# Keys' turn, scaled activations and head outputs kept in PSUM, and two weight tiles opened together, at the seams of a two-block transformer kernel

## The reference, cut to what matters

```python
# layer a: differential attention, 8 heads of 2*128
q, k, v, gate = split(rms_norm(x, a_norm) @ a_w_in, 4);  q, k = partial_rope(q), partial_rope(k)
w = softmax(q0 k0) - lam * softmax(q1 k1)
o = rms_norm(w @ v, subln) * (1 - lambda_init) * silu(gate)
x = x + o @ a_w_out
# shared keys and values, then layer b: window attention with sinks, 32 query heads, 4 key heads
k, v = split(rms_norm(x, kv_norm) @ w_kv, 2);  k = partial_rope(k)
q, gate = split(rms_norm(x, b_norm) @ b_w_in, 2);  q = partial_rope(q)
o = sink_softmax(q k) @ v
x = x + (o * silu(gate)) @ b_w_out
# second block: three branches, then
mix = (g_a * (y_a @ w_a) + g_b * (y_b @ w_b) + g_c * (y_c @ w_c)) @ w_out      # "mix_out"
```

## Time and profile before

| | before |
|---|---|
| median of 3 runs | 2703.34 us |
| the profiled execution: its own time | 2707.28 us |
| its span in the profile | 2705.2 us |
| busy PE / DVE / ACT / POOL | 2604.6 / 997.0 / 1205.1 / 1889.8 us |
| granted PE clock, mean | 0.979 |
| moved by DMA | 425.62 MB, 157 GB/s |

### The profile page before, as it was taken

How to read it: one execution, slowest core, us unless ns; L and a number is a source line. 1 busy time by engine, 2 the same in 40 slices (tenths; PEclk the granted TensorE clock), 3 DMA queues, 4 the chain that set the end, 5 groups by cost and what they waited for, 6 DMA issues and landing times.

```text
span 2705.2 us, 57178 instructions
## 1 busy us (share of the span) xinstructions
PE 2604.6 (96%) x23930; PEld 2519.5 (93%) x23930; DVE 997.0 (37%) x1394; ACT 1205.1 (45%) x1435; POOL 1889.8 (70%) x786
## 2 busy tenths in 40 slices
PE   6999999998999999999999999999799999999996
PEld 5999999898998999999898999999699999999996
DVE  3444444326666341124434443250431130220412
ACT  3444444454666655444434352433343343443432
POOL 3766677676665787556566665888388888888884
PEclk8999999999999999899999999999899999999998
DMA  4555455454444566444444444566266666666663
GB/s 166 155 150 149 148 155 154 130 171 132 135 148 133 165 186 204 138 131 142 131 143 144 130 146 120 171 202 185 74 186 185 182 187 187 186 184 184 182 188 105
DMA packets 120024, 425.62 MB, mean 157 GB/s; under 512 B 12672, under 2 KB 18944, under 8 KB 119552
## 3 DMA queue, kind: packets, MB, share of 16 engines
q1 hardware_dynamic: 115104, 416.54, 51.9%
q10 hardware_dynamic: 4704, 5.77, 0.7%
HBM read 418.07 MB, written 4.19 MB: 156 GB/s over the span
## 4 chain that ended last, share of the span: by engine, by line
PE 92%; DVE 4%; ACT 2%; issue 1%; DMA 0%; SPq 0%; ACTq 0%; DVEq 0%
PE ps L218 20%; PE ps L220 20%; PE ps L227 20%; PE ps L272 16%; PE ps L1814 3%; PE ps L263 3%; PE ps L259 2%; PE ps L258 2%; PE ps L1107 2%; ACT wh L199 1%; DVE og L376 1%; DVE hl L304 1%; PE ps L790 1%; PE ps L1706 1%; PE ps L1708 1%
## 5 line engine op out<-in xcount | busy, mean ns | idle before, releaser
L2529 POOL TENSOR_TENSOR wl<-raw,wh 128x1024 fp32r<-128x1024 f32 x782 | 1889.6, 2438 | 781.3 <-ACT wh L199 780.7
L199 ACT ACTIVATE wh<-raw 128x2048 fp32r<-128x2048 f32 x391 | 748.0, 1913 | 667.9 <-PE ps L227 430.6
L218 PE MATMUL ps<-hh,wh 128*128 128x256 f32 (+1 forms) x3184 | 793.1, 287 | 30.8 <-DVE hl L304 26.6
L220 PE MATMUL ps<-hl,wh 128*128 128x256 f32 (+1 forms) x3184 | 789.2, 286 | 0.0
L218 PEld LDWEIGHTS ps<-hh,wh 128*128 128x128 f32 x3184 | 607.0, 191 | 37.8 <-issue 20.0
L220 PEld LDWEIGHTS ps<-hl,wh 128*128 128x128 f32 x3184 | 608.8, 191 | 0.0
L227 PE MATMUL ps<-hh,wl 128*128 128x256 f32 (+1 forms) x3184 | 418.1, 284 | 0.0
L227 PEld LDWEIGHTS ps<-hh,wl 128*128 128x128 f32 x3184 | 399.5, 189 | 0.0
L218 PE MATMUL ps<-gh,wh 128*128 128x256 f32 x1264 | 303.2, 281 | 0.0
L220 PE MATMUL ps<-gl,wh 128*128 128x256 f32 x1264 | 302.9, 281 | 0.0
L218 PEld LDWEIGHTS ps<-gh,wh 128*128 128x128 f32 x1264 | 239.1, 189 | 0.6 <-issue 0.6
(11 more groups left out here) (374 smaller groups left out, 2949.4 us busy)
## 6 DMA issues: line engine op xcount, KB each, us to landing
raw<-weights SPq DMA_DIRECT2D x782, 512.0 KB, 3.6
xT<-tokens SPq DMA_DIRECT2D x1, 2176.0 KB, 8.7
spill<-xT ACTq DMA_DIRECT2D x1, 2048.0 KB, 14.3
xT<-spill ACTq DMA_DIRECT2D x1, 2048.0 KB, 8.9
out<-xT SPq DMA_DIRECT2D x1, 2048.0 KB, 7.5
C<-consts SPq DMA_DIRECT2D x1, 2000.0 KB, 11.9
arena<-lora ACTq DMA_DIRECT2D x4, 384.0 KB, 3.2
P<-params SPq DMA_DIRECT2D x1, 125.0 KB, 12.8
```

The source lines that it names most:

```text
L199: nc.scalar.activation(wh[:, m % 2, :, :].rearrange("p a b -> p (a b)"), raw[:, 2 * (m % 2):2 * (m % 2) + 2, :, :].rearrange("p a b c -> p ...
L218: nc.tensor.matmul(acc[0:m, 0:n], wh[:, slot, kt, 0:m], rh[:, kt, 0:n], start=(kt == kts[0]), stop=False)
L220: nc.tensor.matmul(acc[0:m, 0:n], wh[:, slot, kt, 0:m], rl[:, kt, 0:n], start=False, stop=False)
L2529: nc.gpsimd.tensor_tensor(wl[:, s // 2, h, :], raw[:, s, :, :], wh[:, s // 2, h, :].bitcast(F32), ALU.subtract)\
```

## The change

1. **Two tiles open each output product** (`a_out`, `b_out`, `mix_out`). `opening_two` issues feature blocks 0 to 11 of tile 0, the same of tile 1 (in bank 1), then blocks 12 to 15 of tile 0 and of tile 1. For `mix_out` it replaces the plain tile.
2. **End of layer a.** `o` is written in place in PSUM, and `og` is made from PSUM. In the last head DVE subtracts quarter 1 before sqs, and quarter 2 right after var. ACT's order is as it was.
3. **`kv` to `b`.** The scaled activations go to PSUM (`Standing`: banks 4 and 5 for quarters 0, 2 and 3, banks 2 and 3 for quarter 1), so L304 subtracts from PSUM. The keys are turned in PSUM banks 0 and 1, the sine table lies in bank 6. Quarter 2 is subtracted before the shuffle and quarter 3 after the turn. ACT makes all copies to `kd`. New waits: `kv` tiles 2 and 3 on l1, quarters 2 and 3 of `gain` on l0 and l2, `b` tile 0 on radd.
4. **Last step of layer b.** PE issues the whole gate tile, then feature blocks 0 to 7 of tile 0 of `b_out`, before the transposes, and blocks 8 to 11 after them. DVE multiplies the gate (`gate`) before it needs the exponentials; ACT does Silu and the rounding of `b_out` tile 1 before its copy of the transposed weights (`wx`). Steps wx, g and gate get semaphores of their own.

```diff
+        def opening_part(pe, phase_name, t, acc, rh, rl, n, split, kts):
+            q = FIRST[phase_name] + t
+            pe.wait_ge(hi_done, q + 1)
+            for kt in kts:
+                if kt % split.size == 0:
+                    pe.wait_ge(split.V.sem, split.V.at(f"l{kt // split.size}"))
+                nc.tensor.matmul(acc[:, 0:n], wh[:, q % 2, kt, :], rh[:, kt, 0:n], start=(kt == 0), stop=False)
+                nc.tensor.matmul(acc[:, 0:n], wh[:, q % 2, kt, :], rl[:, kt, 0:n], start=False, stop=False)
+            for kt in kts:
+                if kt % 8 == 0:
+                    pe.wait_ge(lo_done, 2 * q + kt // 8 + 1)
+                ins = nc.tensor.matmul(acc[:, 0:n], wl[:, q % 2, kt, :], rh[:, kt, 0:n], start=False,
+                                       stop=(kt == 15))
+            return ins
+        def opening_two(pe, phase_name, accs, rh, rl, n, split, begun=False):
+            for kts in (range(12), range(12, KT)):
+                for t, acc in enumerate(accs):
+                    if begun and t == 0 and kts[0] == 0:
+                        continue
+                    ins = opening_part(pe, phase_name, t, acc, rh, rl, n, split, kts)
+                    if kts[-1] == KT - 1:
+                        ins.then_inc(tile_done, 1)
@@ attn_a_dve, last head @@
                 if ends:
                     split_ao.quarter_dve(dve, 0)
+                    split_ao.quarter_dve(dve, 1)
                 dve.wait_ge(A.sem, A.at("sqo", i))
...
                 if ends:
-                    split_ao.quarter_dve(dve, 1)
+                    split_ao.quarter_dve(dve, 2)
...
-                if ends:
-                    split_ao.quarter_dve(dve, 2)
-                        out=fa["o"][:, d, :], in0=ps[:, 6 + d, 0:NT], scalar=p("subln", d), in1=fa["rstd"],
+                        out=ps[:, 6 + d, 0:NT], in0=ps[:, 6 + d, 0:NT], scalar=p("subln", d), in1=fa["rstd"],
@@ kv_pe, tiles 2 and 3 @@
+                    pe.wait_ge(split_b.V.sem, split_b.V.at("l1"))
@@ gain in kv_act @@
+                if k >= 2:
+                    act.wait_ge(split_b.V.sem, split_b.V.at("l0" if k == 2 else "l2"))
+                    ins = nc.scalar.activation(gained[k][:, j, :], xT[:, kt, 0:SEQ], ACT.Copy, scale=p("b", kt))
@@ kv_dve @@
+            turned, sine = ps[:, 0:2, 0:NT], ps[:, 6, 0:NT]
+            nc.vector.tensor_tensor(sine, c("sin_b"), factor_b.out, ALU.mult)
             split_b.quarter_dve(dve, 1)
+            split_b.quarter_dve(dve, 2)
...
-            nc.vector.tensor_tensor(sh, sh, both(f2["sinr"]), ALU.mult)
+            nc.vector.tensor_tensor(sh, sh, both(sine), ALU.mult)
-            nc.vector.tensor_tensor(x, x, both(f2["cosr"]), ALU.mult)
+            nc.vector.tensor_tensor(turned, turned, both(f2["cosr"]), ALU.mult)
-            nc.vector.tensor_tensor(x, x, sh, ALU.add)
+            nc.vector.tensor_tensor(x, turned, sh, ALU.add)
-            for e in range(2):
-                kd_copy(nc.vector.tensor_copy, V, 0, e)
-            split_b.quarter_dve(dve, 2)
             split_b.quarter_dve(dve, 3)
@@ attn_b_pe @@
-                for k in range(4):
+                for k in range(6 if ends else 4):
+                    ins = part(pe, "b", n, k, ps[:, 1, :], hh, hl, SEQ)
+                if ends:
+                    ins.then_inc(tile_done, 1)
+                    opening_part(pe, "b_out", 0, ps[:, 0, :], gh, gl, SEQ, split_bo, range(8))
...
+                if ends:
+                    opening_part(pe, "b_out", 0, ps[:, 0, :], gh, gl, SEQ, split_bo, range(8, 12))
```

More of the change, by code:

```diff
@@ L306, in dve, with __init__, quarter_act, quarter_dve @@
                         .then_inc(self.V.sem, self.V.step(f"l{k}"))
+        class Standing(Split):
+            def __init__(self, name, places, pair, n):
+                Split.__init__(self, name, None, pair, n)
+                self.places = places
+            def quarter_act(self, eng, V, count, k):
+                f = slice(4 * k, 4 * k + 4)
+                eng.wait_ge(V.sem, count)
+                nc.scalar.activation(self.pair[0][:, f, 0:self.n], self.places[k], ACT.Copy)\
+                    .then_inc(self.A.sem, self.A.step(f"h{k}"))
+            def quarter_dve(self, eng, k):
+                f = slice(4 * k, 4 * k + 4)
+                eng.wait_ge(self.A.sem, self.A.at(f"h{k}"))
+                nc.vector.tensor_tensor(self.pair[1][:, f, 0:self.n], self.places[k],
+                                        self.pair[0][:, f, 0:self.n].bitcast(F32), ALU.subtract)\
+                    .then_inc(self.V.sem, self.V.step(f"l{k}"))
         class Norm:
@@ L1040, in kv_act @@
                     act.wait_ge(V.sem, V.at("radd"))
-                    for e in range(2):
-                        kd_copy(lambda o, i_: nc.scalar.activation(o, i_, ACT.Copy), A, 1, e)
+                    for h in range(2):
+                        for e in range(2):
+                            kd_copy(lambda o, i_: nc.scalar.activation(o, i_, ACT.Copy), A, h, e)
         def kv_dve(dve):
@@ L1242, in attn_b_dve, with gate @@
             dve.wait_ge(SK["v"].sem, SK["v"].at("table"))
+            def gate(s):
+                dve.wait_ge(tile_done, done("b", 2 + 2 * s - (s == STEPS_B - 1)))
+                nc.vector.tensor_tensor(f2["gb"][:, s % 2, :], ps[:, 1, 0:256], f2["rs"][:, 0:256], ALU.mult)\
+                    .then_inc(SGB["v"].sem, SGB["v"].step("gate"))
             for s in range(STEPS_B):
+                ends = s == STEPS_B - 1
                 at = P_AT["sinks"][0] + 2 * s
@@ L1262, in attn_b_dve @@
                     .then_inc(V.sem, V.step("sn"))
+                if ends:
+                    gate(s)
                 dve.wait_ge(A.sem, A.at("es", s))
@@ L1278, in attn_b_dve @@
                     .then_inc(V.sem, V.step("w2"))
-                dve.wait_ge(tile_done, done("b", 2 + 2 * s - (s == STEPS_B - 1)))
-                nc.vector.tensor_tensor(f2["gb"][:, s % 2, :], ps[:, 1, 0:256], f2["rs"][:, 0:256], ALU.mult)\
-                    .then_inc(V.sem, V.step("gate"))
+                if not ends:
+                    gate(s)
                 if s in (6, 10, 14):
@@ L1288, in attn_b_dve @@
             split_bo.quarter_dve(dve, 3)
-        b_out = Product("b_out", "b_out", (gh, gl), SEQ, xT, add=True, split=split_bo, after="zz")
+        b_out = Product("b_out", "b_out", (gh, gl), SEQ, xT, add=True, split=split_bo, after="zz",
+                        begun=True)
         two = TwoNorms("two", ("fin", "mix_pre"), SEQ, b_out.blocks(),
```

78 lines of the change are left out of this document (44 added, 34 removed).

## The result

| | before | after |
|---|---|---|
| median | 2703.39 us (4 runs, 2701.4 to 2706.2) | 2677.45 us (4 runs, 2675.5 to 2678.8) |
| the profiled execution: its own time | 2707.28 us | 2678.78 us |
| its span | 2705.2 us | 2676.9 us |
| busy PE / DVE / ACT / POOL | 2604.6 / 997.0 / 1205.1 / 1889.8 | 2594.4 / 978.5 / 1205.8 / 1886.4 |
| granted PE clock, mean | 0.979 | 0.985 |

The ratio of after to before is 0.9901, with a 95% interval of 0.9889 to 0.9914: 25.9 us faster by the medians, 28.3 by the two spans. Forecast were 27.0 us and 2676.3 us.

A forecast was written before the change was run, and what follows sets the result against it. PE was taken as the bound (92% of the chain), plus its stops and half clock. Gains 11.1 + 6.9 + 6.2 + 3.0 = 27.2, less 0.2, give 27.0 off 2703.34: 2676.3 us, range 2671.5 to 2682.5.

The forecast's parts named there:

- The first rival: DVE and POOL still exclude each other with PSUM forms: kv to b gains only 4.4 us, total 2683.0 us; 6%.
- the term for the product with the values: Last step of layer b: the product with the values takes half of 2.64 us, ending at 878.5.
- The longer wait for sqs: End of layer a: PE waits 3.4 instead of 1.19 us, as quarter 1's subtraction now precedes sqs.
- The clock's loss: End of layer a: half clock after PE's stop loses 1.5 to 3.3 us, taken as 2.0.
- the third rival: End of layer a gains nothing, its longer stop and cold start eating 3 us: total 2679.3 us; 8%.
- the lower bound: End of layer a: if the 3.4 us stop counts as a cold start, the gain is 1.7 us.
- The wait for ACT at the third tile: At each two-tile opening PE waits 0.7 to 0.9 us for ACT's rounding of tile 2's upper weights.
- the wait for POOL's second half: Tile 2's second half comes from POOL 4.8 us after the upper part against PE's 4.7: 0.2 us off the sum.
- The second rival: Tile 2 of each product waits for POOL, up to 2.4 us three times: gain 20, total 2683.5 us; 6%.
- the refill loop: Slower rival: weight slots' refill (10.6 us per two tiles against PE's 11.3) becomes the bound; at 6 us landing 2712; 3%.

The follow-up runs named there:

- kv_sbuf: Changed kernel with scaled activations, turned keys and sine table back in SBUF between kv and b, new order and ACT copies kept: 2676.33 us (5 runs).
- a_order: Changed kernel with the subtraction of quarter 1 at the end of layer a moved behind sqs, before var: 2674.47 us (4 runs).
- kv_both: Changed kernel with activations, keys' turn and sine in SBUF and the first half of the kd copies on DVE before quarter 3: 2686.23 us, one run.
- no_fill: Changed kernel with the last step of layer b as before the change, b_out still opened by two tiles: 2684.47 us (7 runs).
- mix_one: Changed kernel with mix_out opened by one plain tile as before the change: 2683.79 us (9 runs).
- a_one: Changed kernel with a_out opened by one plain tile, DVE's new order kept: 2681.53 us, one run.
- best2: Changed kernel with quarter 1 subtracted behind sqs in layer a, and b_out's opening reordered to complete tile 0 earlier: 2674.66 us (5 runs).
- b_one: Changed kernel with tile 1 of b_out made after tile 0, the last softmax still filled: 2677.66 us, one run.

## Why the prediction was right

**kv to b, 11.1 forecast, 10.9 measured.** The steps held: `b` starts when `kv` ends, turned forms at 0.72 us (0.75 forecast), no half clock. The quarter came 5.7 us early (5.6 forecast), the copies on ACT took 3.04 us (3.2). The first rival is out in both its halves. The PSUM forms don't run into POOL, and kv_sbuf shows that its price was wrong too: with SBUF forms the new order lost 1.4 us, not 6.7. The rival charged 3.3 us for each of the two quarters and 8.7 for the turn, 15.3 in all; in kv_sbuf they took 1.2, 1.2 and 7.8, and DVE's slack held the difference to the PSUM forms. That POOL and two SBUF inputs meet is shown: 2.10 to 2.92 us against 0.72 for the three products, and 1.83 against 0.42 for one step of the query's turn whose operands are the same. It costs POOL too: the four halves that the prediction reads at 2.7 us each take 2.4 each after (9.60 us from 602.18), where no such instruction of DVE meets them. The Trainium skill, page "SBUF — State Buffer", section "SBUF: two separate sides", ties this to instructions that take both inputs from SBUF; the trace agrees. Copies with one SBUF input are held in these traces as well: 2.35 us for 64x32 elements, which take 0.17 undisturbed.

**Last step of layer b, 6.9 forecast, 6.4 measured.** The mechanism held: PE waits 0.18 us at the transposes and keeps its clock. The step that failed is the term for the product with the values, "half of 2.64". The 40 matmuls of 2.64 us in the earlier trace rows are two things under one line: 20 of the product with the values in the step before the last, up to 256 columns each, and then the 20 narrower ones of the last step's scores. So half of the row is not the product. Its 20 alone take 1.9 us from their start to the next instruction's, after (861.87 to 863.75) as well as before, where they start at 879.85 with 1.95 us. So 0.6 us too little was charged, and that is the missing 0.5. The last quarter landed at 867.1 without being waited for. The moved copy on ACT costs nothing that PE sees, as forecast. Undone alone the filling costs 7.2 us, more than the whole gain of 6.4, and the second tile 4.1, so they overlap as the parts of `kv` do.

**mix_out, 6.2 forecast, 6.3 measured.** 12.1 us for two tiles, 11.3 plus a wait of 0.65 for the upper weights.

**End of layer a, 3.0 forecast, 3.5 measured.** The longer wait for sqs was forecast at 3.4 us and is 3.39. The clock's loss was forecast at 2.0 us of a possible 1.5 to 3.3; 3.4 us at 0.53 is a loss of 1.6. What is gained against it are the waits of 3.06 and 1.29 us in the opening before, and a second half-clock stretch of 3.4 us that followed the first of them; the prediction has both only in its end mark of 510.8. So the third rival is out, and so is the lower bound that was tied to the Trainium skill, page "TensorE: Matmul & The Clock Gate", section "What's actually happening": this place was no long cold start. In a_order the clock didn't fall at all here.

**The wait for ACT at the third tile** was forecast at 0.75 to 0.8 us and is 0.56, 0.66 and 0.65. What the third tile loses inside, the wait for POOL's second half, was put at 0.2 us in all. Against a tile of 5.69 us at 256 columns the third takes 6.07 in `b_out` and 5.89 in `mix_out`, so 0.4 and 0.2: that term was too small as well. The second rival (2.4 us three times) and the refill loop are out; ACT waited 3.82 us for one load at 880.39, and PE didn't stop for it.

**The sum.** 27.0 us against 25.9 by the medians is nearer than its parts: `b_out` came 0.5 us short and the end of layer a 0.5 us over, and these cancel. With runs of one kernel 3 to 12 us apart, a median within 1.2 us of the forecast is in part luck.

What was tested by undoing: the PSUM operands, the copies, the two-tile opening at each product, the filling, and the order of sqs; the order in `kv` only together with the copies and the scaled activations. The undone places cost 9.4, 7.2, 6.5 and 2.3 us (kv_both, no_fill, mix_one, a_one), 25.4 in all. `o` in PSUM at the end of layer a was not tried by itself.

## What to carry to other kernels

When a stall has several causes on one engine, undo them singly and together: here two parts cost 1.4 and 0 us alone and 9.4 together, and either credit, taken alone, would be wrong. Count the slack of the engine before pricing a slower instruction, and take a duration from the very step that moves, not from its neighbour or from a row that merges two things. Opening a product with two tiles is worth about what the last part of its input is late, and costs some 0.65 us of refill and up to 0.4 inside the third tile; what comes first in that opening must be re-tuned for each place, since the order that gained at one seam lost at another.

## What the runs showed of the hardware

PE's clock also falls where PE never stops. In the second block stands a run of small matmuls (4x128, 128x128) that takes 12.7 us at full clock, with PE busy all the time. In the changed kernel's profile the granted clock drops to 0.50 6.3 us into it, for 17.1 us, 5 of them under full-sized matmuls; after POOL the columns are clock, DMA share, GB/s:

```profile
1120.00:1130.00 10.00, 10.00 (x33) 7.42 (x32) 0.64 (x2) 0.00 (x0) 0.00 (x0) 0.50 0.11 41
1130.00:1140.00 10.00, 10.00 (x70) 10.00 (x70) 3.49 (x12) 5.51 (x18) 0.63 (x1) 0.79 0.00 0
```

The same work in the profile of no_fill:

```profile
1120.00:1130.00 10.00, 10.00 (x56) 7.60 (x56) 0.00 (x0) 2.08 (x3) 4.65 (x2) 1.00 0.58 172
```

From the third tile of `b_out` to that of `mix_out` it makes 926.9 us against 920.3, and 919.3 in kv_sbuf. It was there in 12 of the 14 profiles looked at, those of before and after among them, for 13.7 to 20.5 us, and not in those of kv_sbuf and no_fill. Why it comes in some executions and not in others is open. Some 7 us of the spread in the totals can come from it. The whole spread goes with the mean granted clock of each run: before's 2688.8 to 2705.5 us in 11 runs with 0.986 to 0.980, and best2's 2665.9 to 2677.6 with 0.990 to 0.986.

The length of a stop alone doesn't say whether the clock falls. Before, the stop of 1.19 us for sqs was followed by 3 us at 0.50. In a_order the same stop of 1.19 us is followed by full clock:

```profile
490.00:495.00 5.00, 4.54 (x33) 4.06 (x32) 4.91 (x5) 3.27 (x4) 0.89 (x1) 1.00 0.02 3
```

In a_one PE stops for 2.85 us before 501.47 and goes on at full clock; in b_one a stop of 3.38 us before 867.39 is followed by 3.4 us at 0.50.
